# An S5 layer whose column products hold taps and powers stationary and whose result returns through memory in channel order

## The reference

```python
def _s5_scan(u, h_re, h_im, ...):
    lam_bar = jnp.exp(lam * dt)
    ...
    bu = jnp.einsum('blgc,gpc->blgp', u_blk, b_bar)
    bu = bu.at[:, 0].add(lam_bar * h)
    _, hs = lax.associative_scan(_linear_combine, (a, bu), axis=1)
    y = jnp.real(jnp.einsum('blgp,gcp->blgc', hs, c_c)) + d_g * u_blk
...
ag = jax.nn.gelu(y).astype(x.dtype) @ w['w_glu'][o]
mix = ag[..., :D_MODEL] * jax.nn.sigmoid(ag[..., D_MODEL:])
x = x + mix
x = x + _hmoe(_rmsnorm(x, w['norm_ffn'][l]), ...)   # 32 experts, top 2 of one group of 8
```

## Time and profile before

| | |
|---|---|
| median of 3 runs | 1092.79 us (1092.39 to 2146.93) |
| the profiled execution | 1091.85 us, its span 1090.0 us |
| busy share of the span | PE 87%, PE weight load 53%, DVE 38%, ACT 17%, POOL 34% |
| the stretch of the S5 layer's products and the GLU | 598 to 729 us |

### The profile page before, as it was taken

How to read it: one execution, slowest core, us unless ns; L and a number is a source line. 1 busy time by engine, 2 the same in 40 slices (tenths; PEclk the granted TensorE clock), 3 DMA queues, 4 the chain that set the end, 5 groups by cost and what they waited for, 6 DMA issues and landing times.

```text
span 1090.0 us, 15860 instructions
## 1 busy us (share of the span) xinstructions
PE 950.8 (87%) x5716; PEld 577.3 (53%) x5716; DVE 416.2 (38%) x913; ACT 182.8 (17%) x353; POOL 375.8 (34%) x647
## 2 busy tenths in 40 slices
PE   3999989899897888787788499999989999787786
PEld 3788879545554444444444466444455555344342
DVE  5301155757752222232227762123465223221217
ACT  5311021222210000000016421102351000000003
POOL 1278900283256666656551730000020221101000
PEclk9999999899898999999999789999979999999998
DMA  7126860650669999999994744703047999999965
GB/s 257 39 78 218 295 259 3 254 183 20 247 265 395 423 420 416 421 402 409 393 364 145 110 107 182 328 29 146 19 182 275 421 421 424 423 424 425 425 270 214
DMA packets 45920, 292.39 MB, mean 268 GB/s; under 512 B 10609, under 2 KB 12017, under 8 KB 26391
## 3 DMA queue, kind: packets, MB, share of 16 engines
q1 hardware_dynamic: 35463, 270.29, 62.8%
q0 software_dynamic: 8640, 16.03, 3.9%
q10 hardware_dynamic: 1760, 5.31, 1.5%
HBM read 270.47 MB, written 36.80 MB: 282 GB/s over the span
## 4 chain that ended last, share of the span: by engine, by line
PE 56%; DMA 28%; DVE 6%; SPq 4%; issue 3%; POOL 2%; ACT 1%; POOLq 0%; DVEq 0%; ACTq 0%
DMA arena<-in_w_gu 18%; PE ps L739 13%; PE ps L863 10%; PE ps L1007 9%; PE ps L1204 5%; DMA arena<-in_w_down 4%; PE ps L997 3%; SPq L570 2%; DMA arena<-scratch_hd,idx_now 2%; PE ps L934 2%; PE ps L1162 2%; PE ps L1158 2%; DMA arena<-scratch_kp 2%; PE ps L893 2%; POOL arena L2345 2%
## 5 line engine op out<-in xcount | busy, mean ns | idle before, releaser
L1007 PE MATMUL ps<-arena 128*64 128x256 f32 x2048 | 239.1, 389 | 52.8 <-DMA arena<-in_w_gu 52.6
L1007 PEld LDWEIGHTS ps<-arena 128*64 128x64 f32 x2048 | 148.5, 140 | 143.9 <-DMA arena<-in_w_gu 44.7
L2246 POOL TENSOR_TENSOR arena<-arena 128x32 f32<-128x32 f32 (+5 forms) x232 | 117.5, 506 | 171.3 <-DMA arena<-in_s_d 73.8
L2345 POOL TENSOR_TENSOR arena<-arena 128x256 f32<-128x256 f32 (+3 forms) x192 | 132.7, 691 | 41.7 <-POOL arena L2345 41.4
L739 PE MATMUL ps<-arena 128*128 128x260 f32 x640 | 141.7, 383 | 0.0
L997 PE MATMUL ps<-arena 128*64 128x512 f32 x512 | 124.7, 631 | 13.8 <-DMA arena<-in_w_down 13.2
L739 PEld LDWEIGHTS ps<-arena 128*128 128x128 f32 x640 | 121.1, 190 | 18.7 <-issue 0.4
L863 PE MATMUL ps<-arena 128*128 128x512 f32 x256 | 118.7, 616 | 3.9 <-DVE arena L1770 3.7
L1989 DVE TENSOR_TENSOR arena<-arena,ps 128x128 f32<-128x128 f32 x64 | 18.3, 288 | 256.2 <-ACT arena L1454 256.1
L1454 ACT ACTIVATE arena<-ps 128x128 f32<-128x128 f32 x64 | 17.8, 278 | 467.8 <-PE ps L1007 467.8
L863 PEld LDWEIGHTS ps<-arena 128*128 128x128 f32 x256 | 48.6, 196 | 61.2 <-issue 60.1
(11 more groups left out here) (225 smaller groups left out, 975.1 us busy)
## 6 DMA issues: line engine op xcount, KB each, us to landing
arena<-in_w_gu SPq DMA_DIRECT2D x64, 2048.0 KB, 13.2
arena<-in_w_down SPq DMA_DIRECT2D x64, 1024.0 KB, 14.0
arena<-in_w_in SPq DMA_DIRECT2D x10, 1024.0 KB, 5.9
scratch_yd<-arena SPq DMA_DIRECT2D x2, 4160.0 KB, 18.6
arena<-scratch_yd SPq DMA_DIRECT2D x16, 512.0 KB, 7.3
arena<-in_w_out SPq DMA_DIRECT2D x1, 4096.0 KB, 12.2
scratch_hd<-arena ACTq DMA_DIRECT2D x8, 512.0 KB
arena<-in_w_glu SPq DMA_DIRECT2D x2, 2048.0 KB, 7.7
```

Of the source, the lines that this page charges most:

```text
L1007: mm = pe.matmul(ps[CAP * f:CAP * f + CAP, 2 + s, 0:256], XT[l][:, kc, CAP * s:CAP * s + CAP], WGU[l][i][s][:, kc, 256 * f:256 * f + 256], ...
L2246: step(g_.tensor_tensor(out, a, b, op))
L2345: g_.tensor_tensor(o, x, y, f).then_inc(sem("matrix_steps"), 1)
```

## The change

- `columns` swaps the operands: taps and powers (128 columns) are stationary, inputs and states (72 columns) move. The result has position in chunk and channel on 128 partitions, and chunks along them.
- The taps lie in `KS` and `TT` with the four group quarters innermost, so that one group's 128 stationary columns are four elements (16 bytes) apart. Each of the 16 reads of taps now fills 128 partitions with one row of 2 KB, all on SP's queue. The order of the eight positions in the partitions is reversed (`HX`, `u_out`), and with it POOL's reversed copies of the powers (`BACKR`, `BACKI`) go.
- ACT applies GELU to the product in PSUM and writes `YG_OF`; the copies to `YK` by ACT and DVE and PE's 64 transposes go. The result is written to memory (`gy`) and read back in channel order (`YS`) in three phases, of the output's 128-channel blocks 0 to 3, 4 and 5, 6 and 7: `channels_out` is one write, `channels_in` eight reads of 128 partitions with rows of 1152 or 576 bytes. ACT copies `YS` to `YT` (`in_tiles`).
- `glu` does blocks 0 to 3 for token tiles 0 and 1, then blocks 4 to 7 for both, then the other tiles.

```diff
-    j += [(("zs", 7), "dve"), (("y", 0), "act"), (("y", 1), "act")]
-    for q in range(2, 8):
-        j += [(("y", q), "act" if q < 4 else "dve"), (("yT", q - 2), "act")]
-    j += [(("yT", q), "act") for q in (6, 7)]
+    j += [(("zs", 7), "dve")] + [(("y", q), "act") for q in range(KC)]
     j += [(("gl", 0, i), "dve") for i in range(5)]
...
-        def taps(eng, s, half):
-            rows = kp.rearrange("(j c) (n w) -> c n j w", c=CW, n=2)
-            at = KZERO - KQ * s
-            eng.dma_start(TT[CW * s:CW * s + CW, half], rows[:, half, :, at:at + L * KQ]
-                          ).then_inc(sem(f"taps_in_{half}"), 16)
+        def taps(eng, half):
+            for j in range(8):
+                rows = bass.AP(kp.tensor, CW * j * KROW + KROW // 2 * half, [[KQ, L], [KROW, CW], [1, L * KQ]])
+                eng.dma_start(TT[:, half, j], rows).then_inc(sem(f"blocks_in_{half}"), 16)
+        def channels_out(eng, ph):
+            n = PHASES[ph][1] * SC
+            flat = bass.AP(gy.tensor, P * 8 * SC * PHASES[ph][0], [[8 * n, P], [1, 8 * n]])
+            eng.dma_start(flat, YG_OF[ph].rearrange("p g k n -> p (g k n)")).then_inc(sem("s5_out"), 16)
+        def channels_in(eng, ph):
+            n = PHASES[ph][1] * SC
+            for s in range(L):
+                rows = bass.AP(gy.tensor, P * 8 * SC * PHASES[ph][0] + CW * 8 * n * s, [[n, 8], [8 * n, CW], [1, n]])
+                eng.dma_start(YS[ph][:, s].rearrange("p k n -> p (k n)"), rows).then_inc(sem("blocks_in_0"), 16)
         def taps_of_group(pr, b):
-            return TT[:, pr // 16, 2 * (pr % 4) + b].rearrange("p (l q c) -> p q l c", l=L, q=4)[:, pr % 16 // 4]
+            return TT[:, pr // 16, 2 * (pr % 4) + b].rearrange("p (n q) -> p q n", q=4)[:, pr % 16 // 4]
...
-            return by_group(X[:, t, :]), HX[:, :, t, :], by_group(GB)
+            return by_group(X[:, t, :]), HX[:, :, TILES - 1 - t, :], by_group(GB)
...
             sp.wait_ge(sem("taps_ready"), 1)
-            sp.dma_start(kv[:, :, KZERO:KROW // 2], KS.rearrange("p n l w -> p n (l w)")).then_inc(sem("taps_out"), 16)
-            sp.wait_ge(sem("taps_out"), 16)
+            sp.dma_start(kv[:, :, KZERO:KROW // 2], KS.rearrange("p n l w -> p n (l w)")).then_inc(sem("s5_out"), 16)
+            sp.wait_ge(sem("s5_out"), 16)
             ring.wait_full(sp, "zs", 3)
-            for s in range(L):
-                taps(sp, s, 0)
+            taps(sp, 0)
             ring.wait_full(sp, "zs", 7)
-            for s in range(L // 2):
-                taps(sp, s, 1)
+            taps(sp, 1)
+            ring.wait_emptied(sp, "y", 3)
+            channels_out(sp, 0)
+            load(WGL[0][:, 0:4], T["w_glu"][0][:, 0:4], "w_in_0")
+            sp.wait_ge(sem("states_in"), 2)
+            sp.wait_ge(sem("s5_out"), 32)
+            channels_in(sp, 0)
+            ring.wait_emptied(sp, "y", 5)
+            channels_out(sp, 1)
+            sp.wait_ge(sem("states_in"), 4)
+            sp.wait_ge(sem("ends_ready"), 3)
+            sp.wait_ge(sem("s5_out"), 48)
+            sp.wait_ge(sem("blocks_in_0"), 256)
+            channels_in(sp, 1)
             sp.wait_ge(sem("ends_ready"), 4)
             sp.dma_start(T["s5_p"], HEND).then_inc(sem("stored"), 16)
             sp.dma_start(T["s5_sr"], SHR).then_inc(sem("stored"), 16)
             sp.dma_start(T["s5_si"], SHI).then_inc(sem("stored"), 16)
-            ring.wait_full(sp, "y", 3)
-            load(WGL[0][:, 0:4], T["w_glu"][0][:, 0:4], "w_in_0")
-            ring.wait_full(sp, "y", 7)
+            ring.wait_emptied(sp, "y", 7)
+            channels_out(sp, 2)
             load(WGL[0][:, 4:8], T["w_glu"][0][:, 4:8], "w_in_1")
+            sp.wait_ge(sem("s5_out"), 64)
+            sp.wait_ge(sem("blocks_in_0"), 384)
+            channels_in(sp, 2)
             load(WGL[1], T["w_glu"][1], "w_out_in")
-            ring.wait_full(sp, "yT", KC - 1)
+            sp.wait_ge(sem("s5_by_act"), 5)
             for s in range(2):
                 load_gate_up(1, s, 0, s)
             for b in range(2):
...
                 if q % 4 == 0:
-                    pe.wait_ge(sem(f"taps_in_{q // 4}"), 16 * L)
+                    pe.wait_ge(sem(f"blocks_in_{q // 4}"), 16 * 8)
                     pe.wait_ge(sem("ends_ready"), 1)
                 if q in (0, 4, 6):
                     pe.wait_ge(sem("states_in"), (1, 3, 4)[q // 3])
                 o = slot("y", q)
                 for j in range(4):
                     pr = 4 * q + j
-                    outs = [o[0:SC, b, j * P:(j + 1) * P] for b in range(2)]
+                    outs = [o[:, b, j * SC:(j + 1) * SC] for b in range(2)]
                     for b in range(2):
-                        pe.matmul(outs[b], U[:, 2 * pr + b, NS:UC], taps_of_group(pr, b), start=True, stop=False)
+                        pe.matmul(outs[b], taps_of_group(pr, b), U[:, 2 * pr + b, NS:UC], start=True, stop=False)
                     for h_, g_ in ((HR, GR), (HI, GI)):
                         for b in range(2):
                             half = slice(64 * b, 64 * b + 64)
-                            mm = pe.matmul(outs[b], h_[half, pr], g_[half, pr, 1:L + 1], start=False, stop=h_ is HI)
+                            mm = pe.matmul(outs[b], g_[half, pr, 1:L + 1], h_[half, pr], start=False, stop=h_ is HI)
                 full(mm)
-            def turned(kc):
-                ring.wait_emptied(pe, "y", kc)
-                o = slot("yT", kc)
-                at = (kc % 4) * P
-                transposes(("yT", kc), [(o[:, l // 4, (l % 4) * SC:(l % 4 + 1) * SC],
-                                         YK[kc // 4][0:SC, l, at:at + P]) for l in range(L)])
             in_chunks(0)
             in_chunks(1)
...
             driven(7)
-            columns(0)
-            for q in range(1, 8):
+            for q in range(KC):
                 columns(q)
-                if q >= 2:
-                    turned(q - 2)
-            turned(6)
             def glu(i, kcs=range(KC)):
                 o = slot("gl", 0, i)
...
-                    if i == 0:
-                        ring.wait_emptied(pe, "yT", kc)
+                    if i == 0 and phase_of(kc)[1] == 0:
+                        pe.wait_ge(sem("s5_by_act"), phase_of(kc)[0] + 3)
                     if i == 0 and kc % 4 == 0:
                         pe.wait_ge(sem(f"w_in_{kc // 4}"), 16 * 5 + 16)
                     for b in range(2):
@@ -1205,10 +1218,11 @@
                                        WGL[0][:, kc, b * 512:(b + 1) * 512], start=kc == 0, stop=kc == KC - 1)
                 if kcs[-1] == KC - 1:
                     full(mm)
-            glu(0, range(4))
-            turned(7)
-            glu(0, range(4, KC))
-            for i in range(1, 5):
+            for i in range(2):
+                glu(i, range(4))
+            for i in range(2):
+                glu(i, range(4, KC))
+            for i in range(2, 5):
                 glu(i)
             def second_half(q):
...
                 take(act, "k", n)
-                give(act, a.copy(KS[:, n].rearrange("p l (q c) -> p q l c", q=4),
+                give(act, a.copy(KS[:, n].rearrange("p l (c q) -> p q l c", q=4),
                                  slot("k", n)[:, 0, :].rearrange("p (q l c) -> p q l c", q=4, l=L)), "k", n)
...
+                        ins = a.copy(out[64 * (1 - s):64 * (2 - s), b, :, NS:SC], src[64 * b:64 * b + 64, s])
                         if (b, s) != (1, 1):
...
             decays(1)
-            act.wait_ge(sem("taps_out"), 16)
-            ring.wait_full(act, "zs", 7)
-            for s in range(L // 2, L):
-                taps(act, s, 1)
-            def y_out(q):
-                take(act, "y", q)
-                if q == 0:
+            step(a.activation(warm, ident[:, 0:1], ACT.Gelu_apprx_tanh))
+            def gelu(kc):
+                take(act, "y", kc)
+                if kc == 0:
                     act.wait_ge(sem("ends_ready"), 2)
-                step(a.copy(*y_views(q, 0)))
-                give(act, a.copy(*y_views(q, 1)), "y", q)
-            def gelu(kc):
-                take(act, "yT", kc)
-                src = slot("yT", kc)
-                if kc == 0:
+                if kc == 6:
+                    act.wait_ge(sem("ends_ready"), 3)
+                ph, k = phase_of(kc)
+                out = YG_OF[ph][:, :, k].rearrange("p (j b) n -> p b j n", b=2)
+                src = slot("y", kc)[:, :, 0:4 * SC].rearrange("p b (j n) -> p b j n", j=4)
+                step(a.activation(out[:, 0], src[:, 0], ACT.Gelu_apprx_tanh))
+                give(act, a.activation(out[:, 1], src[:, 1], ACT.Gelu_apprx_tanh), "y", kc)
+            def in_tiles(ph):
+                k0, n = PHASES[ph]
+                if ph == 0:
                     act.wait_ge(sem("rotated_by_pool"), 8)
-                if kc == 3:
-                    act.wait_ge(sem("states_in"), 2)
-                step(a.activation(YT[:, kc, 0:SEQ].rearrange("p (i k s) -> p s i k", i=4, s=2),
```

(27 more changed lines are left out.)

26 lines of the change are left out of this document (13 added, 13 removed).

## The result

The changed kernel takes 1119.77 us (median of 4 runs, 1118.22 to 1120.92) against 1092.66 us for the kernel before on the same chip: a ratio of 1.0238, with a 95% interval of 1.022 to 1.0257. I had forecast 1084 us, with a range up to 1100. The profiled execution took 1119.12 us, 27.3 us more than the one before. One execution of the kernel before took 2146.93 us, against 1092.39 to 1092.79 for the other three, and is left out of the comparison.

What follows compares the result with a forecast made beforehand. PE was taken as busy throughout from the column products to the GLU, with time gained reaching the end one to one. Start -5.9, transposes -4.9 and stall +1.7 made -9.1 us: 1084 us, range 1082 to 1100 us.

Steps and rivals of the forecast that it cites:

- the products' clock: Column products on PE: half clock only for the first ones, 2.4 us, then full clock; 40.1 us in all.
- with the clock at 0.50 behind it: Sign of a wrong forecast: a wait of over 3 us before the first GLU product or block 6, then half clock.
- The price at full clock: Column products: an exchanged group takes 0.59 us as before, so the swap is worth nothing by itself.
- that is why I lean to free: PE's loads of taps 16 bytes apart: the stride costs nothing, as a float32 load leaves each element 0.83 ns.
- the rival: Column products: the strided tap load takes double, +13.7 us, 1095.7 to 1099.1 us in all; chance 0.3.
- The start: First column product: at 622.9 us with earlier taps, 5.9 us gained, 2.5 at the other end.
- the states are next: Wait of `columns(0)`: behind the taps come DVE's states at 622.8 us, so earlier taps give at most 6.0 us.
- my worst rate: Reads of the taps at 124 GB/s: half 0 lands at 626.3 us, still 2.5 us earlier than before.
- my rival, whose 1115 us: Reads of the taps: eight engines at 7.8 GB/s each, half 0 at 643 us, 1115 us in all; chance 0.05.
- The return path: Write and reads of the result ahead of the GLU: a stall of 1.7 us, none or 4.3 at the ends.
- It just fits: Phase 2 of the return path: copies done at S + 58.5 us, S the products' start; PE needs it at S + 59.6.
- The transposes: PE's transposes between products and GLU, and the eighth block within the GLU: 4.9 us gone.

Runs made afterwards that it cites:

- e_contig: The changed kernel with the 128 tap columns of a product lying together in place of 16 bytes apart (wrong numbers): 1115.19 us.
- e_swap_before: The kernel before with only the operands of its column products exchanged, taps read from columns that lie together (wrong numbers): 1122.91 us.
- e_warm: The changed kernel with twelve products of 512 moving columns put into PE's wait ahead of the first column product: 1126.96 us.
- e_oldorder: The changed kernel with the operands of its column products as before, tap columns still 16 bytes apart (wrong numbers): 1098.55 us.
- e_old_contig: The changed kernel with the operands of its column products as before and the tap columns lying together (wrong numbers): 1089.30 us.
- b_taps8: The kernel before with only the changed reads of the taps, walked 8 by 16, and the order of `U` they need: 1091.82 us in rounds, ratio 0.9976.
- b_taps16: `b_taps8` with the source rows of the taps walked 16 by 8 (wrong numbers): 1087.02 us.
- e_72: `b_taps8` with each column product cut to 72 of its 128 moving columns, under 72 stationary ones (wrong numbers): 1098.97 us.
- e_wide: `e_contig` with 128 moving columns per product in place of 72, 64 of them read twice (wrong numbers): 1097.96 us.

## Why the prediction was wrong

**The failed step is the products' clock.** I wrote that "eight at 37.7 us, plus 2.4 us for the first ones at half clock" make 40.1 us, and "the gap ahead of them shrinks by 6 us and I take it to cost the same". So I carried the rise of the clock over from the old products to the exchanged ones. They measured 70.4 us at 0.50 throughout. Of the 30.3 us above, the clock is 27.8 (67.9 us without the stride, `e_contig`), the stride 2.5; and the exchange alone cost 29.8 us in `e_swap_before`. Why these products don't get the full clock stays open. None of my rivals had the clock in it, though I had 0.50 in the earlier trace rows before me; "with the clock at 0.50 behind it" stood in my list of signs only as something that a wait would cause. The gap itself shrank from 14.8 to 11.9 us, half of what I had.

**The price at full clock was right.** "Exchanged, a group is [...] 0.59 us again": 0.60 in `e_warm`, for the power groups; a tap group without the stride was never seen at full clock. The old operands in the changed kernel needed 40.4 us of the forecast 40.1.

**The stride was mis-sized, and hidden.** My "that is why I lean to free" failed, and the rival was right: at full clock a tap group takes 0.48 us more than a power group in `e_warm` and 0.45 in `e_oldorder`, where the strided operand is the moving one. Over the 32 pairs that is 12.8 us (53.2 of `e_oldorder` against 40.4 of `e_old_contig`), for which the rival had 13.7. At half clock 2.5 us were left of it. Had the clock risen, the change would most likely still have been a loss, which no run shows with its own operands: `e_oldorder`, with the stride on the moving side and the full clock, at 1098.55 us, lies in the rival's forecast of 1095.7 to 1099.1. The Trainium skill (SBUF — State Buffer, "Door 1: The DMA port swizzle") states both a penalty below two hits per 16-byte line and that four float32 can be strided for free; these rows agree with the first.

**The start was short by one waiter.** My "the states are next" was wrong: next was the PSUM slot, 2.1 us behind the states. The most to be had was 3.8 us, not 6.0, and `b_taps8` had it. In the changed kernel the taps took 0.9 us more than even that, with reads at 147 GB/s; half 0 landed at 627.8 us, 18.5 us behind SP's first issue, where my worst rate has 18.9 and the rate of 172 GB/s 14.2.

**Eight engines: the rule holds, its price was mild.** The share of 0.50 and the 0.98 of the 16 by 8 walk are what eight and sixteen engines would give, and so agree with the rule of the Trainium skill (DMA: Bandwidth & Descriptors, "Why a DMA increments its semaphore by 16 and not by 1"). On eight engines each moved 18 GB/s (147 / 8) and not the 7.8 of my rival, whose 1115 us are near the result by accident. The number of partitions mattered as I had read it from the write: on sixteen engines the reads into 128 partitions ran at 269 GB/s (`b_taps16`), those into 16 at 124.

**The return path was right in phase 0 and short in phase 2.** There was no stall in the changed kernel, since PE was late. In `e_old_contig`, with S its first product at 625.78 us, the write landed at S + 27.6 (I had 27.3), ACT's copies began at S + 39.0 (39) and the GLU at S + 42.1 (41.8): the stall of 1.70 us, where I had 1.7, is no luck. Phase 2 came at S + 61.6 and not S + 58.5, for which I had said "It just fits"; it cost 1.57 us. The second half of the weights, which were to "land well ahead of their users", cost 0.34.

**The transposes** were worth what I said: with them 44.2 us and 0.8 in the GLU, without them 40.4; 4.6 us, where I had 4.9.

**The sum.** I had 9.1 us less. The start came 5.0 us later than forecast (2.0 for the later end of the first MoE, 2.1 for the slot, 0.9 for the taps), the products took 30.3 us more, and the stall of 1.7 us was not there. Two terms I did not have: the GLU, which lost the 0.8 us of transposes and yet grew by 0.6, so 1.4 us, about what its first products at half clock cost (0.90 from 698 to 712 us), and 1.4 us in the router and the second MoE, whose cause I have not looked for. -9.1 + 5.0 + 30.3 - 1.7 + 1.4 + 1.4 = 27.3 us, the difference of the two profiled executions.

## What to carry to other kernels

An exchange of the operands keeps the arithmetic, and here it cost the clock that TensorE was granted. Before taking a duration at full clock for a new form, look in the trace for a series of that form, alike in both operands and as long, and ask at which clock it ran; `driven`, with the same 72 moving columns, would have misled. Where there is none, the lower clock is a rival with a price. When a wait is to be taken away, list all waits that end behind it, PSUM slots included. A stride whose cost does not show may only be hidden behind a slower clock.

## What the runs showed of the hardware

- Column products in float32 with 72 moving columns under 128 stationary ones ran 70 us at a granted clock of 0.50, with PE busy throughout, and fell from 1.00 to 0.50 after 6 us when entered at full clock (`e_warm`). Under 72 stationary ones they stayed at 0.50 for 51 us (`e_72`). With 128 moving columns under 128 stationary ones the clock came back after 17 us (`e_wide`), under 72 stationary ones after 5 to 6 (the kernel before, `e_oldorder`, `e_old_contig`, `b_taps8`). `driven`, 72 moving under 64 with a few transposes, came to 1.00 after some 5 us.
- A stationary operand with its columns 16 bytes apart: 1.08 us per group of four records at full clock against 0.60 for products with contiguous loads; 1.14 against 1.06 at half clock. As the moving operand 1.04 against 0.59 at full clock.
- The reads walked 8 by 16, at half the DMA share, came at two rates in executions of one and the same kernel, as stretches of `b_taps8` and of its second profile show, from 622 to 627 us:

```profile
622.00:627.00 5.00, 1.94 (x12) 1.49 (x12) 4.30 (x8) 0.00 (x0) 2.90 (x4) 0.50 0.53 201
```

```profile
622.00:627.00 5.00, 0.00 (x0) 0.00 (x0) 4.64 (x5) 0.00 (x0) 4.07 (x4) 0.50 0.53 149
```

  The second profile started its products at 628.88, released by the taps. What sets the rate stays open.
